# A decoder layer on eight cores: convolution chunks and the sample's pieces between attention steps, gate product first, squares on either engine

## The chip, the cores and the metric

The kernel runs as one program on the 8 cores of one Trainium2 chip. Each core takes one of the 8 prompts (2,048 tokens) and 16 of the 128 sample tokens, and holds its whole share of the work; the cores exchange nothing. The metric is the device time of the slowest core, in microseconds (us). Five engines of a core run side by side, each with an instruction list of its own: TensorE (PE: matmuls), ScalarE (ACT: functions such as Silu, Ln, Exp, Square, which need one of several function tables), VectorE (DVE), GpSimd (POOL: here it only issues the weights' DMAs) and SyncE (SP: issues the other DMAs). A semaphore orders one engine's work behind another's.

## What is computed

One layer, on the tokens of the prompt and on the sample's. `token_mixer` has a gated linear attention (GLA) with a 64x128 state per head, beside a short gated convolution:

```python
h = x + 0.5 * rms_norm(swiglu(rms_norm(x, ng[0]), f1_gate, f1_up, f1_down), ng[1])
mix, s_new, conv_new = token_mixer(rms_norm(h, ng[2]), s0, conv0, w_in, w_gate_up, b_gate,
                                   gla_norm_g, conv_w, w_out)
h = h + rms_norm(mix, ng[3])
h = h + 0.5 * rms_norm(swiglu(rms_norm(h, ng[4]), f2_gate, f2_up, f2_down), ng[5])
gate = jax.nn.sigmoid(rms_norm(h, ng[6]) @ w_ple_gate)
h = h + rms_norm((p @ w_ple_proj) * gate, ng[7])

# swiglu: (silu(x @ w_gate) * (x @ w_up)) @ w_down
# GLA per token: S_t = diag(a_t) S_{t-1} + k_t^T v_t, o_t = q_t S_t; the prompts start with S = 0
# conv group: cb * sum_j conv_w[j] * (cc * ch)[t - 2 + j]; out = concat(gla, conv) @ w_out
```

d_model is 1024, the swiglu's inner width 2816, 4 heads, all in float32. Outputs are h of prompt and sample and the new GLA and convolution states of both.

## The kernel before

**Tiles and streams.** Tokens lie along the free axis, channels along the 128 partitions. A core's 2,064 tokens are 6 tiles of 344, so a matmul of the big products is 128x128 by 344 columns. Two streams, A (tiles 0, 2, 4) and B (tiles 1, 3, 5), go through the stages at the same time, a pass being one tile of each; the names of their buffers end in A and B. The sample's 16 tokens are the last columns of tile 5, so stream B has them in the third pass.

**Stages of a tile.** ffn1 (`ffn`, f=0); the mixer (gates; convolution chunks `conv_chunk` 0 to 3; keys and queries; values; attention over three chunks of up to 128 tokens; output projection); ffn2 (`ffn`, f=1); the embedding stage (`ple`). Between stages stands `boundary` (L725): 8 norm-sum matmuls are closed, `rsq` makes 1/sqrt with an Ln and an Exp on ScalarE, `add_pair` adds the branch to h on VectorE (two operations on 688 columns), then for each pair of channel blocks a Square of h (688 columns) and two scalings with the norm's weights (344 columns each) run on ScalarE, and TensorE takes each pair as it comes (two sums with a matrix of ones `csr`, then its part of the next stage's first products, `feed`). `evac` (L768) empties a product's bank in the same way: Square, then Identity with a scale, both on ScalarE. In the embedding stage `xprep` prepares the next tile's x for its first norm (Square on ScalarE, scaling on VectorE) and TensorE sums its 8 squares with 8 matmuls.

**What sets the order.** The program is written by a planner that runs before the kernel is built. `P.op` puts work of ScalarE and VectorE on a list of pending operations; `pick` (L185) takes from it the one that its cost model would start first, with a surcharge (SWITCH) for a change of function table and the priority `P.prio` as tie break. The main loop (L1422) gives TensorE to the stream whose operands are planned to be there, with the streams' lead deciding ties. Where the planner sees TensorE idle for over 0.6 us it adds matmuls on constants, `warm` (L485), named `ps_bank<-sb_csr 128x344` and recorded at L496, 0.6 of the planned idle time at 0.157 us each. Their results are not used. Once written, each engine's order is fixed, and an instruction waits for its semaphores there.

**Weights.** Both streams use the same weights, which go through a ring in SBUF, `wring`: `pump` (L588) issues blocks from GpSimd in a fixed list (`ffn_w`, `mix_w`, `ple_w`) up to 20 ahead, and a block's place is free when the slower of the streams has released it. While the sample's GLA states lie in the ring (the list's last blocks of `mix_w`, `sg`), `S.pin` (L1095) keeps the ring from moving on.

**Start.** x of both tiles (`load_h`) and the constants (`ngl`, the norms' weights, among them) come over SP's queue; the third weight block waits for x (`gate0`). SP issues in the order in which the planner took them from the list.

**Attention and the sample.** For each chunk: `step_a` (scores: 4 matmuls, mask on VectorE, key transposes), `step_c` (outputs and the new state, which goes over ScalarE and VectorE into `Sr` and `Sst`), `step_d` (norm of the outputs). `gla_done` makes a stream's attention wait for the other's, as it takes over its state. One convolution chunk stands between steps of passes 1 and 2 and two after them. In the third pass all `2 * NS` pieces of `sample_gla` (L1181) come ahead of the first step: a piece is a group of small matmuls `sb_xnB,sb_sqB 128x256` (k times v of the sample) or `sb_WB,sb_wring 128x2` (q times the state), with VectorE's update of the state in the ring between them.

## Time and profile before

| | us |
|---|---|
| median of 3 runs | 1646.17 (1643.25 to 1696.57) |
| the profiled execution, device time | 1645.65 |
| its span, slowest core (core 1) | 1644.0 |
| spans of the 8 cores | 1631.0 to 1644.0 |

| engine | busy us | share | instructions |
|---|---|---|---|
| TensorE | 1537.0 | 93% | 9454 |
| ScalarE | 736.5 | 45% | 1437 |
| VectorE | 715.9 | 44% | 1421 |
| GpSimd | 268.5 | 16% | 512 |

How to read it: the span is the time from the first to the last instruction of the core with the trace shown, and the runs' times are those of the slowest core. The granted clock of TensorE is given as a share of full speed (2.4 GHz), averaged over a stretch; its two levels are 1.0 and half of that (1.2 GHz). A busy TensorE at half clock does half the work, so what a stretch loses is its idle time and, besides, its width times what the clock lacks of 1.

### The profile page before, as it was taken

Reading aid. Unit: us, or ns where it says so; the run is one execution under the profiler, and the core shown is the slowest. Engines: PE = TensorE matmul, PEld = TensorE weight load, DVE = VectorE, ACT = ScalarE, POOL = GpSimd, SP = SyncE. Lnnn points to the kernel's source line nnn. Section 1 sums busy time; section 2 is a strip of 40 time slices with the busy share of each in tenths; the row PEclk is TensorE's granted clock in tenths of the full one; section 3 lists DMA queues with packets and bytes.
Section 4 is the critical chain, followed back from the end, with each engine's and each line's share of the span. In section 5 each row is a group of like instructions: output and inputs, shape, how many; then the busy total and the mean of one; then the engine's idle time right before and its main releaser. Section 6 shows DMA issues by size and latency. Waiting matters only on the chain.

```text
span 1644.0 us, 27962 instructions; the slowest of 8 cores (1631.0 to 1644.0 us)
## 1 busy us (share of the span) xinstructions
PE 1537.0 (93%) x9454; PEld 1492.4 (91%) x9454; DVE 715.9 (44%) x1421; ACT 736.5 (45%) x1437; POOL 268.5 (16%) x512
## 2 busy tenths in 40 slices
PE   6999999899998999999989999799998998999996
PEld 5999889889997999989989999799998997889995
DVE  3331464543324643155554422573315754433136
ACT  3112665642147611275574124841138474511266
POOL 3211210112121221111112112022111110111110
PEclk9999999999998999998999999899999995999998
DMA  9865843468666796565446668399556443566661
GB/s 282 255 186 160 233 142 102 112 181 250 186 193 191 208 328 209 170 184 167 102 156 208 200 176 249 112 279 319 177 160 202 137 142 100 158 177 175 203 190 69
DMA packets 83452, 305.39 MB, mean 186 GB/s; under 512 B 9538, under 2 KB 12498, under 8 KB 82548
## 3 DMA queue, kind: packets, MB, share of 16 engines
q0 software_dynamic: 73040, 283.97, 58.4%
q1 hardware_dynamic: 10276, 19.65, 3.7%
q8 instruction: 80, 1.31, 0.3%
q14 instruction: 56, 0.46, 0.1%
HBM read 292.83 MB, written 10.75 MB: 185 GB/s over the span
## 4 chain that ended last, share of the span: by engine, by line
PE 79%; DMA 7%; ACT 6%; DVE 4%; issue 4%; DVEq 0%; SPq 0%; ACTq 0%; POOLq 0%; POOL 0%
PE ps_bank L472 78%; DMA sb_wring<-f2a 3%; DMA sb_wring<-f2b 2%; ACT L519 2%; DMA sb_wring<-f1b 1%; ACT sb_xnB L519 1%; DVE sb_hB L522 1%; DVE sb_xnB L522 1%; DMA sb_ngl<-ngl 1%; ACT sb_ta L519 1%; PE ps_bank L496 1%; ACT sb_WA L519 1%; PE ps_bank L504 0%; ACT sb_sqB L519 0%; DVE sb_WA L527 0%
## 5 line engine op out<-in xcount | busy, mean ns | idle before, releaser
L472 PE MATMUL ps_bank<-sb_xnA,sb_wring 128*128 128x344 f32 x2208 | 410.6, 332 | 19.0 <-DVE sb_WA L527 8.6
L472 PE MATMUL ps_bank<-sb_xnB,sb_wring 128*128 128x344 f32 x2208 | 396.6, 323 | 6.6 <-ACT sb_xnB L519 5.7
L472 PEld LDWEIGHTS ps_bank<-sb_xnA,sb_wring 128*128 128x128 f32 x2208 | 370.1, 197 | 27.2 <-issue 26.0
L472 PEld LDWEIGHTS ps_bank<-sb_xnB,sb_wring 128*128 128x128 f32 x2208 | 358.2, 190 | 13.5 <-issue 13.1
L472 PE MATMUL ps_bank<-sb_WA,sb_wring 128*128 128x344 f32 x1872 | 330.7, 323 | 11.4 <-DVE sb_WA L527 4.7
L472 PE MATMUL ps_bank<-sb_WB,sb_wring 128*128 128x344 f32 (+1 forms) x1904 | 333.7, 320 | 1.7 <-DVE sb_wring L522 1.0
L472 PEld LDWEIGHTS ps_bank<-sb_WA,sb_wring 128*128 128x128 f32 x1872 | 301.6, 189 | 17.8 <-issue 17.5
L472 PEld LDWEIGHTS ps_bank<-sb_WB,sb_wring 128*128 128x128 f32 x1904 | 309.1, 190 | 2.6 <-issue 2.4
L607 POOL DMA_DIRECT2D sb_wring<-f2a x132 | 69.7, 528 | 367.1 <-PE ps_bank L472 334.9
L519 ACT ACT_TABLE_LOAD x91 | 116.8, 1283 | 27.4 <-DMA sb_ngl<-ngl 14.4
L607 POOL DMA_DIRECT2D sb_wring<-f1a x132 | 69.7, 535 | 290.7 <-PE ps_bank L472 280.7
L519 ACT ACTIVATE sb_tg0A<-sb_tg0A 128x344 f32<-128x344 f32 x78 | 38.2, 490 | 158.5 <-DVE sb_tg0A L522 158.1
L519 ACT ACTIVATE sb_tg1A<-sb_tg1A 128x344 f32<-128x344 f32 x78 | 38.2, 490 | 155.9 <-DVE sb_tg1A L522 155.7
L522 DVE TENSOR_TENSOR sb_tg1A<-ps_bank,sb_rsA 128x344 f32<-128x344 f32 x84 | 43.3, 516 | 120.0 <-PE ps_bank L472 109.0
L522 DVE TENSOR_TENSOR sb_tg0A<-ps_bank,sb_rsA 128x344 f32<-128x344 f32 x84 | 43.3, 515 | 110.7 <-PE ps_bank L472 110.6
L519 ACT ACTIVATE sb_sqA<-ps_bank 128x344 fp32r<-128x344 f32 x72 | 32.9, 457 | 119.0 <-PE ps_bank L472 118.7
L519 ACT ACTIVATE sb_tg0B<-sb_tg0B 128x344 f32<-128x344 f32 x78 | 38.2, 490 | 97.6 <-DVE sb_tg0B L522 97.6
L519 ACT ACTIVATE sb_sqB<-ps_bank 128x344 fp32r<-128x344 f32 x72 | 32.7, 455 | 99.1 <-PE ps_bank L472 93.5
L522 DVE TENSOR_TENSOR sb_sqA<-sb_sqA 128x344 fp32r<-128x344 f32 x36 | 18.6, 518 | 126.6 <-ACT sb_sqA L519 125.1
L472 PE MATMUL ps_bank<-sb_sqB,sb_csr 128*128 128x344 f32 (+2 forms) x155 | 47.7, 353 | 26.4 <-ACT sb_sqB L519 12.3
L519 ACT ACTIVATE sb_tg1B<-sb_tg1B 128x344 f32<-128x344 f32 x78 | 38.3, 491 | 69.9 <-DVE sb_tg1B L522 69.8
L522 DVE TENSOR_TENSOR sb_sqB<-sb_sqB 128x344 fp32r<-128x344 f32 x36 | 18.6, 517 | 107.6 <-ACT sb_sqB L519 106.6
(198 smaller groups left out, 1647.6 us busy)
## 6 DMA issues: line engine op xcount, KB each, us to landing
sb_wring<-f1a POOLq DMA_DIRECT2D x132, 512.0 KB, 10.0
sb_wring<-f2a POOLq DMA_DIRECT2D x132, 512.0 KB, 5.5
sb_wring<-f1b POOLq DMA_DIRECT2D x48, 704.0 KB, 5.5
sb_wring<-f2b POOLq DMA_DIRECT2D x48, 704.0 KB, 5.3
sb_wring<-wca POOLq DMA_DIRECT2D x24, 512.0 KB, 6.8
sb_wring<-wo POOLq DMA_DIRECT2D x24, 512.0 KB, 5.6
sb_wring<-wpg POOLq DMA_DIRECT2D x24, 512.0 KB, 7.3
sb_wring<-wg POOLq DMA_DIRECT2D x12, 512.0 KB, 6.7
```

Source lines behind the costliest of these rows:

```text
L472: ins = e.matmul(out.ap, a.ap, b.ap, start=(first and i == 0), stop=(last and i == n_ - 1))
L496: ins = e.matmul(out.ap, a.ap, b.ap, start=True, stop=True)
L519: P.op("act", lambda e: e.activation(out=out.ap, in_=in_.ap, func=func, **kw), reads=rd, writes=[out], table=table)
L522: P.op(eng, lambda e: e.tensor_tensor(out=out.ap, in0=in0.ap, in1=in1.ap, op=op), reads=[in0, in1], writes=[out])
L607: P.op("pool", (lambda o, s: lambda e: e.dma_start(out=o.ap, in_=s))(dst, src), reads=gate0 if i == 2 else (), writes=[dst], dma=f"ws{i % ...
```

## The change

**Who does a square or a scaling.** An operation on the pending list may have two ways, on ScalarE or VectorE (`sqr`, `scl`). The planner takes the way that starts first by its model, with a term `late` for the later one. `boundary`, `evac`, the first norm, the convolution's first tap and `xprep` use them. Exp with scale -0.5, the second half of each 1/sqrt, gets 20 more priority (`PAIR`), so that it follows its Ln more closely.

**Order of products.** In `ffn` the gate's product is first and the up product second, and the gate's own operations are pending before the up product is issued. In the mixer the values come ahead of keys and queries (the `vrow` block is moved up as it is); `mix_w` has the blocks in the new order; one buffer (`Einv`) and the softplus values (`sps`) move to other places.

**Between attention steps.** Convolution chunk 1 leaves its place ahead of the keys, so that three chunks (1 to 3) stand between the attention steps or right behind; in the third pass all three stand ahead of the attention. Of the sample's pieces one (`FIRST`) is done before the wait for `gla_done` and up to 6 (`EACH`) in each of the attention's steps. What `sample_gla` keeps moves from `sq` to a free part of `xn`.

**Sums of x.** `xprep` adds its squares in pairs on VectorE, and TensorE sums 2 vectors per tile and not 8. **Start.** What is pending is written out before the constants are asked for, and the planner's model has a transfer time for SP's large loads.

```diff
+FIRST = 1
+EACH = 6
+PAIR = 20.0
...
+                o.due = [self.ready(w[0], o.reads, o.writes) for w in o.ways]
+            for way, (eng, fn, kw) in enumerate(o.ways):
+                due, free = o.due[way], self.free[eng]
+                t = max(due, free)
+                tab = kw.get("table")
+                turn = SWITCH if tab is not None and tab != self.table else 0.0
+                late = max(0.0, t - min(max(d, self.free[w[0]]) for d, w in zip(o.due, o.ways)))
+                key = (t + turn if due > free + 0.15 else free, due - o.prio + turn + late)
+                if best is None or key < best[0]:
+                    best = (key, t, o, way)
...
+            elif writes and ndma == 1 and width > 400:
+                self.link = max(self.link, start + 2.0) + 0.0018 * width
+                self.done[tok] = self.link + 0.5
...
+            if func == AF.Exp and scale == -0.5:
+                P.prio += PAIR
...
+        def sqr(out, in_):
+            P.op("act", lambda e: e.activation(out=out.ap, in_=in_.ap, func=AF.Square), reads=[in_], writes=[out],
+                 other=("dve", lambda e: e.tensor_tensor(out=out.ap, in0=in_.ap, in1=in_.ap, op=ALU.mult), {}))
+
+        def scl(out, in_, g):
+            P.op("act", lambda e: e.activation(out=out.ap, in_=in_.ap, func=AF.Identity, scale=g.ap), reads=[in_, g], writes=[out],
+                 other=("dve", lambda e: e.tensor_scalar(out=out.ap, in0=in_.ap, scalar1=g.ap, scalar2=None, op0=ALU.mult), {"dur": 0.4}))
...
         def mix_w(smp):
             o = halves(wg_d, 0) + halves(wg_d, 1)
-            for c in range(2):
-                o += halves(wca_d, c) + [(wcb_d, c, 0, 1024)]
+            o += halves(wca_d, 0) + [(wcb_d, 0, 0, 1024)]
+            o += [(wv_d, 0, 0, 2048), (wv_d, 1, 0, 2048)]
             o += halves(wkq_d, 0) + halves(wkq_d, 1)
-            o += [(wv_d, 0, 0, 2048), (wv_d, 1, 0, 2048)]
-            for c in range(2, 4):
+            for c in range(1, 4):
...
-                act(q, hp, AF.Square)
+                sqr(q, hp)
                 for k in range(2):
-                    act(xv(S, c + k, n), hv(S, c + k, n), AF.Identity, scale=gvec(gpre, c + k))
+                    scl(xv(S, c + k, n), hv(S, c + k, n), gvec(gpre, c + k))
...
-            act(raw(S, m, n), bank.v(0, n), AF.Identity, scale=gvec(g, m, half))
+            scl(raw(S, m, n), bank.v(0, n), gvec(g, m, half))
...
-                bu_ = yield from prod(S, n, fA_d[f], j, 1024)
                 bg_ = yield from prod(S, n, fA_d[f], j, 0)
...
+                later(gate)
+                bu_ = yield from prod(S, n, fA_d[f], j, 1024)
+
...
-            yield from conv_chunk(S, T, 1)
...
             if last_pass:
-                for c in range(2, 4):
+                for c in range(1, 4):
                     yield from conv_chunk(S, T, c)
...
-            done_c = 4 if last_pass else 2
+            done_c = 4 if last_pass else 1
...
             if ns:
-                go = True
-                for _ in range(2 * NS):
-                    if go:
-                        go = yield from piece()
-            prev = None
+                for _ in range(FIRST):
+                    go = yield from piece()
+            while T.idx > 0 and not gla_done[T.idx - 1]:
+                yield None
             for s in range(nch):
-                lo, hi = T.chunks[s]
-                yield pe([wv_(S, T, "kt", 0, 2 * n), wv_(S, T, "qtz", 0, 4 * n)])
-                am = step_a(s)
+                yield from prep(s)
                 if prev is not None:
                     step_d(*prev)
                 if done_c < 4:
                     yield from conv_chunk(S, T, done_c)
                     done_c += 1
-                yield pe([am.v(0, 512), W.v(o["kz"], o["kz"] + 512), Sr[gk["k"] % 2].v(0, 256)])
-                bo, oq = step_c(s, am)
+                for _ in range(EACH):
+                    if go:
+                        go = yield from piece()
+                kb, k0 = kz_at(s)
+                yield pe([ams[s], kb.v(k0, k0 + 512), Sr[gk["k"] % 2].v(0, 256)])
+                bo, oq = step_c(s, ams[s])
                 prev = (s, bo, oq)
+            while go:
+                go = yield from piece()
             for c in range(done_c, 4):
...
-            kept = S.sq.v(0, 512, 0, NS, r=True)
+            kept = S.xn.v(2048, 2560, 0, NS, r=True)
...
-                q = S.W.v((18 + c % 4) * n, (19 + c % 4) * n, r=True)
-                act(q, xr, AF.Square)
-                ts(S.W.v((10 + c) * n, (11 + c) * n, r=True), xr, gvec(0, c), None, ALU.mult, None)
-                xq.append(q)
+                k = 18 + c if c < 2 else 20 + c % 2
+                sqr(S.W.v(k * n, (k + 1) * n, r=True), xr)
+                scl(S.W.v((10 + c) * n, (11 + c) * n, r=True), xr, gvec(0, c))
+                if c % 2 and c > 1:
+                    acc = S.W.v(18 * n, 20 * n)
+                    tt(S.W.v(18 * n, 20 * n, r=True), acc, S.W.v(20 * n, 22 * n), ALU.add)
 
...
+            xq = [S.W.v((18 + k) * n, (19 + k) * n, r=True) for k in range(2)]
+            bx = yield from hold()
             yield pe(xq, [bx.v(0, n)], True)
-            xsum(0)
+            mm(bx.v(0, n), [(csr.v(C_OD, C_OD + 128, r=True), q) for q in xq])
...
             load_h(streams[0], tiles[0], c)
+        P.settle(list(P.pending))
```

SyncE's list at its beginning (`hA`, `hB` are x of the two streams' first tiles, four loads each of two channel blocks). Before:

```order
L462 DMA sb_hB<-x 128x688 x4
L462 DMA sb_ngl<-ngl 128x64
L462 DMA sb_hA<-x 128x688 x4
L462 DMA sb_cst<-cst 128x392
L462 DMA sb_sm<-sm 128x16
```

Of the change:

```order
L475 DMA sb_ngl<-ngl 128x64
L475 DMA sb_hA<-x 128x688 x4
L475 DMA sb_hB<-x 128x688 x4
L475 DMA sb_cst<-cst 128x392
L475 DMA sb_sm<-sm 128x16
```

The norm's weights `ngl` are now first and stream A's x is ahead of stream B's; what follows is unmoved.

TensorE's list in the third pass, at the end of the sample's pieces and the beginning of an attention step of stream B (`WB` holds its keys and queries, `Sr` the state, `sqB` the masked scores or the sample's keys). Before:

```order
L472 MATMUL ps_bank<-sb_WB,sb_wring 128x2 x4
L472 MATMUL ps_bank<-sb_xnB,sb_sqB 128x256 x4
L496 MATMUL ps_bank<-sb_csr 128x344 x2
L472 MATMUL ps_bank<-sb_WB,sb_wring 128x2 x4
L472 MATMUL ps_bank<-sb_xnB,sb_csr 128x64
L472 MATMUL ps_bank<-sb_WB 128x128 x4
L504 MATMUL ps_bank<-sb_cst,sb_WB 128x128 x2
L472 MATMUL ps_bank<-sb_WB,sb_Sr 128x128
L472 MATMUL ps_bank<-sb_sqB,sb_WB 128x128
```

Of the change, around a piece in the middle of the attention:

```order
L485 MATMUL ps_bank<-sb_WA,sb_wring 128x344 x8
L485 MATMUL ps_bank<-sb_sqA,sb_csr 128x344
L485 MATMUL ps_bank<-sb_WA,sb_wring 128x344 x8
L485 MATMUL ps_bank<-sb_WB,sb_wring 128x2 x4
L485 MATMUL ps_bank<-sb_xnB 128x256 x4
L485 MATMUL ps_bank<-sb_sqA,sb_csr 128x344 x2
L509 MATMUL ps_bank<-sb_csr 128x344 x4
L485 MATMUL ps_bank<-sb_WB,sb_wring 128x2 x4
L485 MATMUL ps_bank<-sb_WB,sb_Sr 128x128
L485 MATMUL ps_bank<-sb_sqB,sb_WB 128x128
```

Before, the pieces stand one behind the other, with fillers (`sb_csr`) between, and then the attention steps. Now stream A's full products (`sb_WA,sb_wring 128x344`) stand between the pieces and the steps.

TensorE's list where stream B goes from ffn2 to the embedding stage for the first time, while stream A is in that stage (`xnB` is the scaled h). Before:

```order
L472 MATMUL ps_bank<-sb_xnA,sb_wring 128x344 x8
L496 MATMUL ps_bank<-sb_csr 128x344 x2
L472 MATMUL ps_bank<-sb_sqA,sb_csr 128x344
L472 MATMUL ps_bank<-sb_WA,sb_csr 128x344
L472 MATMUL ps_bank<-sb_WA,sb_wring 128x344 x2
L472 MATMUL ps_bank<-sb_xnA,sb_wring 128x344 x8
L472 MATMUL ps_bank<-sb_sqA,sb_csr 128x344
L472 MATMUL ps_bank<-sb_WA,sb_csr 128x344
L472 MATMUL ps_bank<-sb_sqB,sb_csr 128x344 x2
L472 MATMUL ps_bank<-sb_xnB,sb_wring 128x344 x2
```

Of the change:

```order
L485 MATMUL ps_bank<-sb_xnA,sb_wring 128x344 x8
L485 MATMUL ps_bank<-sb_sqA,sb_csr 128x344
L509 MATMUL ps_bank<-sb_csr 128x344 x15
L485 MATMUL ps_bank<-sb_sqB,sb_csr 128x344 x2
L485 MATMUL ps_bank<-sb_xnB,sb_wring 128x344 x4
L509 MATMUL ps_bank<-sb_csr 128x344 x6
L485 MATMUL ps_bank<-sb_sqB,sb_csr 128x344 x2
L485 MATMUL ps_bank<-sb_xnB,sb_wring 128x344 x4
L509 MATMUL ps_bank<-sb_csr 128x344 x3
```

Before, four of A's product groups stand in B's passage and two fillers; now fillers do (15, 6 and 3), A's groups follow, and one of A's norm matmuls (`sb_WA,sb_csr`) of each pair is gone with the sums of x.

## Rows read from the trace of the kernel before

**Rows 1.** The page's part 1: busy us, share of the span, instructions.

```profile
PE 1537.0 (93%) x9454; PEld 1492.4 (91%) x9454; DVE 715.9 (44%) x1421; ACT 736.5 (45%) x1437; POOL 268.5 (16%) x512
```

**Rows 2.** Core 1, TensorE by windows: us, busy (instructions), clock, DMA, GB/s.

```profile
0.00:20.00 20.00, 3.88 (x11) 1.00 0.87 242
200.00:260.00 60.00, 54.28 (x334) 0.94 0.45 131
280.00:360.00 80.00, 71.27 (x418) 0.94 0.48 143
500.00:560.00 60.00, 51.31 (x275) 0.89 0.52 164
720.00:760.00 40.00, 34.41 (x185) 0.87 0.40 126
780.00:860.00 80.00, 73.38 (x494) 1.00 0.43 121
1020.00:1060.00 40.00, 30.53 (x158) 0.87 0.51 166
1240.00:1280.00 40.00, 35.17 (x198) 0.91 0.49 155
1340.00:1400.00 60.00, 53.57 (x248) 0.66 0.33 100
1420.00:1560.00 140.00, 132.45 (x817) 1.00 0.62 177
```

**Rows 3.** Timeline, start: start us, us, what [idle before <-releaser].

```profile
2.90 0.85 SPq L462 DMA_DIRECT2D sb_ngl<-ngl  x1
...
12.84 6.87 POOL L607 DMA_DIRECT2D sb_wring<-f1a  x13 [9.57 <-DMA sb_hB<-x]
...
14.40 1.28 ACT L519 ACT_TABLE_LOAD   x1 [14.40 <-DMA sb_ngl<-ngl]
...
16.37 0.63 PE L472 MATMUL ps_bank<-sb_sqA,sb_csr 128*128 128x344 f32 x1 [7.97 <-DVE sb_sqA L522]
```

**Rows 4.** Groups by line, ScalarE and VectorE: busy us, mean ns | idle before.

```profile
L519 ACT ACT_TABLE_LOAD x91 | 116.8, 1283 | 27.4 <-DMA sb_ngl<-ngl 14.4 <-PE ps_bank L472 3.6 <-DVE sb_tg1B L522 3.3
...
L519 ACT ACTIVATE sb_xnB<-sb_hB,sb_ngl 128x344 fp32r<-128x344 f32 x80 | 42.0, 568 | 0.0
...
L519 ACT ACTIVATE sb_sqB<-sb_hB 128x688 fp32r<-128x688 f32 x36 | 27.7, 769 | 3.3 <-DVE sb_hB L522 3.2
...
L522 DVE TENSOR_TENSOR sb_hB<-sb_hB,sb_xnB 128x688 f32<-128x688 f32 x28 | 24.1, 871 | 0.7
...
L534 DVE TENSOR_SCALAR sb_WB<-sb_WB,sb_ngl 128x344 fp32r<-128x344 f32 x16 | 6.3, 395 | 2.8 <-ACT sb_WB L519 2.7
```

**Rows 5.** Timeline, TensorE, first passage from ffn2 to the embedding stage.

```profile
506.65 0.83 PE L472 MATMUL ps_bank<-sb_WA,sb_wring 128*128 128x344 f32 x2 [2.34 <-DVE sb_WA L527]
...
513.84 0.55 PE L472 MATMUL ps_bank<-sb_sqB,sb_csr 128*128 128x344 f32 x2 [1.31 <-ACT sb_sqB L519]
...
527.97 2.63 PE L472 MATMUL ps_bank<-sb_xnA,sb_wring 128*128 128x344 f32 x8 [3.14 <-DVE sb_WA L527]
```

**Rows 6.** Timeline, ScalarE, a table load there and the next activation.

```profile
504.03 1.28 ACT L519 ACT_TABLE_LOAD   x1
...
505.33 0.49 ACT L519 ACTIVATE sb_tg1A<-sb_tg1A 128x344 f32<-128x344 f32 x1
```

**Rows 7.** Timeline, TensorE, the attention step behind the sample's pieces.

```profile
1384.71 0.45 PE L472 MATMUL ps_bank<-sb_WB,sb_Sr 128*128 128x128 f32 x1 [2.07 <-ACT sb_Sr L519]
...
1386.44 1.49 PE L472 MATMUL ps_bank<-sb_WB 128*128 128x128 f32 x8
```

**Rows 8.** Timeline, TensorE, the same kind of step in the first pass.

```profile
289.50 0.22 PE L472 MATMUL ps_bank<-sb_WB,sb_Sr 128*128 128x128 f32 x1
...
290.34 0.61 PE L472 MATMUL ps_bank<-sb_WB 128*128 128x128 f32 x4
```

**Rows 9.** The page's part 5: issues of one kind of weight block, GpSimd.

```profile
L607 POOL DMA_DIRECT2D sb_wring<-f2a x132 | 69.7, 528 | 367.1 <-PE ps_bank L472 334.9
```

126 lines of the change are left out of this document (63 added, 63 removed).

## The prediction

> **What bounds the kernel now.** I read the page's table of engines first. TensorE is busy 1537.0 us in a span of 1644.0, ScalarE and VectorE under half of it [rows 1]. So the kernel is bound by TensorE's work, and what an edit can win is what TensorE loses: its idle time, and what its clock lacks. Full-speed work is already dense: in the long ffn stretch of the last pass 817 matmuls take 132.45 us, 0.162 us each, at clock 1.00 [rows 2].
>
> Then I went through the span in windows and took for each (width - busy) + (1 - clock) x width. The losses lie at few places [rows 2]:
>
> - start, 0 to 20: 20 - 3.88 = 16.1.
> - ffn1 to mixer, three passes (200:260, 720:760, 1240:1280): 5.7 + 3.6, 5.6 + 5.2, 4.8 + 3.6 = 28.5.
> - mixer to ffn2, two passes (280:360, 780:860): 8.7 + 4.8, and 6.6 = 20.1.
> - ffn2 to embedding, two passes (500:560, 1020:1060): 8.7 + 6.6, 9.5 + 5.2 = 30.0.
> - the sample, 1340:1400: 6.4 idle + 0.34 x 60 = 20.4 of clock = 26.8.
> - 1420:1560: 7.5, idle alone, at full clock.
>
> Together 129 us. The timeline of TensorE then tells what ends its waits. In the passage to the embedding stage it waits 2.34, 1.31 and 3.14 us for products and squares on VectorE and ScalarE [rows 5]: a serial chain through both engines, during which ScalarE also changes its function table. At the start the first product waits for x: GpSimd's issues go on at 12.84, behind `hB`; the norm weights `ngl`, issued at 2.90 behind `hB`, let ScalarE begin at 14.40; TensorE starts at 16.37 [rows 3].
>
> **The change, part by part.** Durations come from the profiled execution, so the sum is made against its 1645.65 us (span 1644.0 and 1.65 around it), 0.5 under the median shown, 1646.17.
>
> *Two ways for squares and scalings.* From the two programs' lists: ScalarE's activations fall from 1348 to 1112, VectorE's operations rise from 1423 to 1671. In the lists the function table changes 69 times where it did 91, as Exp now follows its Ln. That is 22 x 1.283 = 28 us less of loads on ScalarE [rows 4]. In a passage (four Squares of 688 columns and eight scalings) ScalarE now needs 4 x 0.77 + 8 x 0.57 = 7.6 us. A pair on VectorE costs 0.87 for the square (two operands, as the 688-column add) and 0.40 per scaling, against 0.77 and 0.57 [rows 4]. Shared between both, a passage's preparation could end 2 to 3 us earlier. But VectorE also has `add_pair` there, 2 x 0.87 x 4 = 7 us, which stands ahead of the squares in the same passage. So I take a good third of the loss at each place: 8.5 of 28.5 at ffn1 to mixer (2.8 a passage), 5 of 20.1 at mixer to ffn2. Bounds: 0 (VectorE's adds set the pace anyway) and 24 (half of both).
>
> *The passage to the embedding stage.* The lists show opposite things. A's norm sums of x shrink: 32 matmuls become 8 over four tiles, 24 x 0.16 = 3.8 us of certain work. But A's groups no longer stand in B's passage; 24 fillers do, which are 24 x 0.162 = 3.9 us of matmuls that compute nothing, written for a planned gap of 24 x 0.157 / 0.6 = 6.3 us. Before, the waits of 2.34, 1.31, 3.14 and shorter ones made 8.7 [rows 2, 5]. So the idle time hardly shrinks, while the fillers hold the clock, of which 6.6 and 5.2 us are lost today [rows 2]. I take 2 us a passage, 4, beside the 3.8. Bounds: 0 and 12.
>
> A rule of the Trainium skill speaks for more. "ScalarE: Activation LUTs", section "What ACT_TABLE_LOAD costs", puts a switch at some 1283 ns for the load plus some 1380 ns of drain. By it 22 fewer switches would be 58 us of ScalarE and not 28. The trace agrees with the first figure and shows no drain of this size: a load begins at 504.03, lasts 1.28, and the next activation starts at 505.33 [rows 6]. By the page's figure the gain at the passages would lie nearer its bound of 24, by the row it stays at 13.5.
>
> *The sample.* Before, all pieces stand in a row, with small matmuls and fillers, and TensorE's clock is at 0.66 over 60 us; the attention's step behind them waits 2.07 us for the state and runs its 8 small matmuls in 1386.44 - 1384.71 = 1.73 us, at half clock, where the same step in pass 1 takes 290.34 - 289.50 = 0.84 [rows 2, 7, 8]. Now A's full products stand between pieces and steps. The waits (2.07 here and a few of 0.5 to 1.3) should mostly go: 4 of the 6.4 idle. Of the clock's 20.4 I take a third, 7: the pieces are still many small matmuls. Sum 11. Bounds: 4, and 20. Three convolution chunks between the attention's steps in passes 1 and 2 fill waits of the same kind; they are in the 5 above.
>
> *The start.* `ngl` first and `hA` ahead of `hB` lets A's norm begin some us sooner. But weight blocks 1 and 2 and the x of both tiles share the same link (DMA share 0.87 over 0:20 [rows 2]), and GpSimd's third block waits for `hB`, which lands later now, so what is won on A is partly lost on the weights. I take 5. Bounds: 0 and 8 (16.37 minus the about 8 us that ngl and A's x need at 242 GB/s: 1.4 MB, 5.8 us, behind an issue at 1 us).
>
> *Gate ahead of up, values ahead of keys.* The same matmuls in another order. Silu gets one product's time (8 x 0.16 = 1.3 us) more; in the dense stretches nothing waits for it, so 0. If that cover is gone (a tight ring of buffers), each costs at most its 0.5 us of Silu. The values need only `xn`, and their evacuation stands in the time in which keys and queries wait for the gates: in the 5 above.
>
> *Fillers.* Their count rises from 121 to 157: 36 x 0.162 = 5.8 us of TensorE. A filler in a true gap is free; where the operands come earlier than planned it delays. I charge half: +3. Bounds 0 and 5.8.
>
> Sum: -5 - 8.5 - 5 - 4 - 3.8 - 11 + 3 = -34.3; 1645.65 - 34.3 = 1611.4, rounded to 1612.
>
> **The rivals.**
>
> 1. *Relief that is off the path.* ScalarE and VectorE are under half busy [rows 1], so less of ScalarE's time need not shorten a chain that goes through both: VectorE's `add_pair` of 7 us sets the pace of a passage, and the stalls move to it. Then of the two-ways edit a quarter is left (3.4 of 13.5), the passage to the embedding stage keeps only its 3.8 less 3 of fillers, the sample gives its waits and little of the clock (6), the start 3: 1645.65 - 3.4 - 0.8 - 6 - 3 = 1632.5. For it speaks that the planner itself still plans 24 fillers into one passage. Against it: TensorE's waits name ScalarE's squares and scalings too [rows 5]. 0.32.
>
> 2. *The clock stays up.* In all windows above the clock's lack is 3.6 + 5.2 + 3.6 + 4.8 + 6.6 + 5.2 + 20.4 = 49.4 us. If fewer and filled gaps keep TensorE at its upper level nearly everywhere, half of this comes back and not the 13 or so that my sum has in it: 12 more and all table relief converts, 10 more: 1590. 0.12.
>
> 3. *VectorE becomes the bound of the passages (slower).* The two ways move onto VectorE some 29 squares of 688 columns and 56 scalings of h: 29 x 0.87 + 56 x 0.40 = 47.6 us, over 18 passages 2.6 each. The planner chooses by its own model of both engines; if the moved work stands ahead of `add_pair` of the other stream or of the gates' products, all of it is on the path: 1645.65 + 47.6 less 13 (start 5, and 8 of the sample) = 1680. It decides when over 46 of the 47.6 us are on the path, so 0.04.
>
> 4. *Weights come late.* The mechanism would be that a scaling on VectorE holds GpSimd's next issue back. Scalings of this kind, SBUF to SBUF, rise from 33 to 87 by the lists; if each held back an issue by its 0.40 us [rows 4], that is 54 x 0.40 = 21.6 us at most, and 1612 + 10 = 1622 if half of them met an issue that TensorE waits for. In the trace the issues take 528 ns on average, and GpSimd's idle time before them is 367 us, 335 of it waiting for TensorE to free the ring [rows 9]: slack. So 0.05. A rule of the Trainium skill stands behind this rival and speaks against the change: "SBUF — State Buffer", section "Who interferes with whom", says that a VectorE tensor_scalar in its two-port mode takes the port pair that it shares with GpSimd, and GpSimd is locked out for the whole instruction. No row of before shows such a lock.
>
> **How the numbers follow.** Main case 0.47 (its own range 1598 to 1625), rival 1 0.32 (1624 to 1642), rival 2 0.12 (1585 to 1598), rival 4 0.05, rival 3 0.04. The predicted time is 1612. The range of 1592 to 1638 leaves out rival 3, the lower half of rival 2 and the top quarter of rival 1, under 0.2. 2% is about what a measurement of this kernel can tell from no change; it lies at 0.98 x 1646.17 = 1613.2. The main case is a little over half below it (0.27), rival 2 all (0.12), rival 4 hardly (0.01): faster 0.40. Only rival 3 reaches 1679, mostly: slower 0.03. Same 0.57.
>
> **What would show it.** In the new profile: TensorE's first product at 11 to 12 us (start). Table loads 69, 89 us in all. The windows at the three kinds of passage with 2 to 3 us less idle time and VectorE busy in them; if the waits there are now for VectorE's `hB` and `xnB`, rival 1 holds. In the sample's part no wait of 2 us for `Sr`, and a clock over 0.75; if it is 0.66 still, 7 us of the sum are missing. Passages to the embedding stage with clock 1.00 and about 8 us of idle and fillers. Waits for `wring` longer than before would show rival 4. The forecast is wrong if the busy time of TensorE doesn't fall, though its waits do: then the clock gave nothing back.

## The result, and the profile after

The changed kernel is slower: 1657.03 us (median of 6 runs) where the kernel before has 1647.38 beside it, ratio 1.0061 with a 95% interval of 1.0039 to 1.0082. That is 10 us more where the prediction had 34 less. The interval is clear of 1, so this is a small loss and not a tie, though one of less than 2%. Its profiled execution has a span of 1651.3 us (core 7). All ratios are taken over the runs in which neither half of the chip ran at a lower clock than the other; e16 and e17 below have no such runs, and for them I give the ratio of cores 0 to 3 alone.

The page's line of engines, of the changed kernel:

```profile
PE 1540.8 (93%) x9466; PEld 1494.7 (91%) x9466; DVE 850.3 (51%) x1669; ACT 603.7 (37%) x1179; POOL 268.9 (16%) x512
```

Beside [rows 1], ScalarE has 133 us less and VectorE 134 us more: the work moved as the lists said. TensorE's busy time (1537.0 before, 1540.8 now) and share did not fall, and nor did all its waits together (88.1 us before, 92.1 now, median of the cores).

TensorE in the windows of [rows 2], of the changed kernel (us, busy, instructions, clock, DMA share, GB/s):

```profile
0.00:20.00 20.00, 7.13 (x23) 1.00 0.80 219
200.00:260.00 60.00, 55.05 (x358) 0.91 0.44 128
280.00:360.00 80.00, 71.63 (x425) 0.94 0.51 150
500.00:560.00 60.00, 54.88 (x327) 0.97 0.70 198
720.00:760.00 40.00, 33.25 (x170) 0.74 0.43 128
780.00:860.00 80.00, 72.72 (x447) 0.94 0.41 109
1020.00:1060.00 40.00, 33.64 (x194) 1.00 0.71 212
1240.00:1280.00 40.00, 32.53 (x163) 0.78 0.46 146
1340.00:1400.00 60.00, 53.53 (x297) 0.86 0.32 93
```

The same account as in the prediction, idle time and clock together, before against after: passages to the embedding stage (500:560, 1020:1060) 30.0 against 5.1 + 1.8 + 6.4 = 13.3. Passages from ffn1 to the mixer (200:260, 720:760, 1240:1280) 28.5 against 10.4 + 17.2 + 16.3 = 43.9. Mixer to ffn2 (280:360, 780:860) 20.1 against 13.2 + 12.1 = 25.3. The sample's window 26.8 against 14.9. By these windows the passages to the embedding stage gained 16.7 us, about twice the 7.8 of the forecast, and the passages around the mixer lost where a gain was forecast.

Fixed windows are blind to work that moves over their edge. So I also took, on all 8 cores, the times at which TensorE issues its n-th 344-column matmul of a weight block (8160 in either kernel), at places where both kernels have done the same work, and the median over the cores of the width of each part:

| from, to (n-th) | what | before | changed | e1: passages on ScalarE |
|---|---|---|---|---|
| 0, 80 | start | 34.4 | 33.3 | 34.5 |
| 960, 1760 | mixer, pass 1 | 190.9 | 194.9 | 191.0 |
| 2560, 2880 | to embedding, pass 1 | 72.9 | 68.8 | 65.9 |
| 3760, 4400 | mixer, pass 2 | 159.7 | 170.9 | 159.8 |
| 5200, 5520 | to embedding, pass 2 | 76.8 | 72.1 | 67.4 |
| 6400, 7120 | mixer and sample, pass 3 | 208.7 | 209.1 | 205.6 |
| 7920, 8159 | end | 51.2 | 54.9 | 50.5 |

The parts left out differ by 1.1 us at most. The loss is in the mixers' passages of passes 1 and 2 (+4.0, +11.2) and at the end (+3.7). The passages to the embedding stage gained 4.1 and 4.7, which is 8.8 and not the 16.7 of the windows. The sample's pass is as long as before: what its window shows as a gain was given back beside it.

What TensorE waits for, in all, of the changed kernel (engine, line waited for: us in total, times, longest):

```profile
PE ps_bank L485 <- DVE sb_sqB L557: 14.7, 8, 3.2
PE ps_bank L485 <- ACT sb_sqB L556: 9.9, 8, 2.0
PE ps_bank L485 <- DVE sb_WA L544: 9.7, 6, 2.7
PE ps_bank L485 <- DVE sb_WB L539: 9.0, 5, 2.1
```

L557 is the VectorE way of `sqr`. Before, the passages had no such wait, and now it is the largest. VectorE's timeline in the second pass's passage from ffn1 to the mixer shows how it comes (changed kernel, core 7):

```profile
719.86 0.87 DVE L539 TENSOR_TENSOR sb_WB<-sb_WB,sb_rqB 128x688 fp32r<-128x688 f32 x1
721.21 0.88 DVE L539 TENSOR_TENSOR sb_hB<-sb_hB,sb_WB 128x688 f32<-128x688 f32 x1 [0.47 <-DVE sb_WB L539]
722.26 0.88 DVE L557 TENSOR_TENSOR sb_sqB<-sb_hB 128x688 fp32r<-128x688 f32 x1 [0.17 <-DVE sb_hB L539]
723.05 0.39 DVE L561 TENSOR_SCALAR sb_xnB<-sb_hB,sb_ngl 128x344 fp32r<-128x344 f32 x1
723.36 2.44 DVE L539 TENSOR_TENSOR sb_WB<-sb_WB,sb_rqB 128x688 fp32r<-128x688 f32 x3
725.72 0.87 DVE L539 TENSOR_TENSOR sb_hB<-sb_hB,sb_WB 128x688 f32<-128x688 f32 x1
726.69 0.88 DVE L557 TENSOR_TENSOR sb_sqB<-sb_hB 128x688 fp32r<-128x688 f32 x1
...
727.91 1.64 DVE L539 TENSOR_TENSOR sb_hB<-sb_hB,sb_WB 128x688 f32<-128x688 f32 x2
```

A square, a scaling and three multiplies stand between the first and the second add to h (the second add needs one of these multiplies), another square between the second and the third. From the first multiply to the last add it takes 729.55 - 719.86 = 9.7 us. The same passage of the kernel before (core 1), first and last row:

```profile
728.90 0.88 DVE L522 TENSOR_TENSOR sb_WB<-sb_WB,sb_rqB 128x688 fp32r<-128x688 f32 x1 [0.69 <-ACT sb_rqB L519]
...
735.69 0.86 DVE L522 TENSOR_TENSOR sb_hB<-sb_hB,sb_WB 128x688 f32<-128x688 f32 x1
```

There it is 736.55 - 728.90 = 7.65 us, with two multiplies and nothing else between the first and the second add. Over all 18 passages of a core, the mean time from the first add to the end of the last is 6.4 us before and 8.3 in the change (median of the cores). What the new order does to the other two engines, changed kernel, ScalarE and then TensorE:

```profile
726.68 1.05 ACT L560 ACTIVATE sb_xnB<-sb_hB,sb_ngl 128x344 fp32r<-128x344 f32 x2 [3.92 <-DVE sb_hB L539]
...
728.91 0.78 ACT L556 ACTIVATE sb_sqB<-sb_hB 128x688 fp32r<-128x688 f32 x1 [1.18 <-DVE sb_hB L539]
```

```profile
723.28 0.91 PE L485 MATMUL ps_bank<-sb_sqB,sb_csr 128*128 128x344 f32 x2 [2.15 <-DVE sb_sqB L557]
...
727.71 0.91 PE L485 MATMUL ps_bank<-sb_sqB,sb_csr 128*128 128x344 f32 x2 [2.37 <-DVE sb_sqB L557]
```

ScalarE, which could have done the square, is idle for 3.92 us because the next h isn't there, and TensorE waits twice, 4.5 us together. Its clock falls with the first of these gaps to the lower level, stays there through the second, and falls once more ten us later (window, busy, instructions, clock, DMA share, GB/s):

```profile
720.00:723.00 3.00, 1.14 (x8) 1.00 1.07 294
723.00:737.00 14.00, 11.32 (x37) 0.51 0.23 78
737.00:747.00 10.00, 8.22 (x54) 1.00 0.43 134
747.00:754.00 7.00, 6.58 (x25) 0.52 0.32 101
```

The mean over 720:760 is 0.74, where it was 0.87.

### The profile page after: what moved, and what is told of

Its sections match the earlier page's. It is cut to its first block, busy times and chain, and to the rows that moved or that the text cites. A ratio compares the mean times of both kernels' runs of the same rounds, so it can differ in the third digit from the quotient of the medians.

```text
span 1651.3 us, 28350 instructions; the slowest of 8 cores (1637.0 to 1651.3 us)
## 1 busy us (share of the span) xinstructions
PE 1540.8 (93%) x9466; PEld 1494.7 (91%) x9466; DVE 850.3 (51%) x1669; ACT 603.7 (37%) x1179; POOL 268.9 (16%) x512
## 4 chain that ended last, share of the span: by engine, by line
PE 79%; DVE 9%; issue 4%; DMA 4%; ACT 3%; DVEq 0%; POOL 0%; ACTq 0%; POOLq 0%
PE ps_bank L485 78%; DVE sb_hB L539 1%; DMA sb_wring<-f2a 1%; DMA sb_wring<-f1b 1%; PE ps_bank L509 1%; DVE sb_xnB L539 1%; DMA sb_wring<-f1a 1%; DVE sb_hA L539 1%; DMA sb_wring<-f2b 1%; DVE sb_tb L544 1%; ACT L535 1%; DVE sb_sqB L557 1%; DVE sb_WB L539 1%; DVE sb_xnB L561 0%; DMA sb_wring<-wpg 0%
## 5 line engine op out<-in xcount | busy, mean ns | idle before, releaser
L485 PE MATMUL ps_bank<-sb_xnA,sb_wring 128*128 128x344 f32 x2208 | 402.7, 327 | 26.4 <-DVE sb_WA L544 8.2
L485 PE MATMUL ps_bank<-sb_xnB,sb_wring 128*128 128x344 f32 x2208 | 406.0, 328 | 4.9 <-DVE sb_WB L544 2.3
L485 PEld LDWEIGHTS ps_bank<-sb_xnA,sb_wring 128*128 128x128 f32 x2208 | 364.2, 193 | 35.5 <-issue 35.0
L485 PEld LDWEIGHTS ps_bank<-sb_xnB,sb_wring 128*128 128x128 f32 x2208 | 367.5, 194 | 9.9 <-issue 9.6
L535 ACT ACT_TABLE_LOAD x68 | 87.2, 1283 | 9.2 <-PE ps_bank L485 4.5
L485 PE MATMUL ps_bank<-sb_sqB,sb_csr 128*128 128x344 f32 (+2 forms) x155 | 51.7, 382 | 33.3 <-DVE sb_sqB L557 14.7
L539 DVE TENSOR_TENSOR sb_tg1B<-ps_bank,sb_rsB 128x344 f32<-128x344 f32 x84 | 43.2, 515 | 60.7 <-PE ps_bank L485 51.0
L539 DVE TENSOR_TENSOR sb_tg0B<-ps_bank,sb_rsB 128x344 f32<-128x344 f32 x84 | 43.2, 514 | 56.3 <-PE ps_bank L485 52.6
L485 PEld LDWEIGHTS ps_bank<-sb_sqB,sb_csr 128*128 128x128 f32 x155 | 29.7, 210 | 44.8 <-issue 44.4
```

The costliest lines, as they stand in the source:

```text
L485: ins = e.matmul(out.ap, a.ap, b.ap, start=(first and i == 0), stop=(last and i == n_ - 1))
L535: P.op("act", lambda e: e.activation(out=out.ap, in_=in_.ap, func=func, **kw), reads=rd, writes=[out], table=table)
L539: P.op(eng, lambda e: e.tensor_tensor(out=out.ap, in0=in0.ap, in1=in1.ap, op=op), reads=[in0, in1], writes=[out])
```

## The experiments

All ratios are to the kernel before, run beside each on the same chip. A hundredth is 16.5 us, and the intervals are about 0.002 (3 us) either way. First, what the loss is.

**e1, passages on ScalarE alone.**

```diff
-                sqr(q, hp)
+                act(q, hp, AF.Square)
...
-                    scl(xv(S, c + k, n), hv(S, c + k, n), gvec(gpre, c + k))
+                    act(xv(S, c + k, n), hv(S, c + k, n), AF.Identity, scale=gvec(gpre, c + k))
```

> The changed kernel with one part undone: in the passages between stages (boundary) squares and scalings are on ScalarE alone, as before; the two ways stay everywhere else. Theory 1 (VectorE's squares and scalings stand between its own adds to h, so the next pair comes later and TensorE waits 2 to 3 us for sqB on VectorE, then runs at half clock): the 14.7 us of waits for VectorE's sqB go, and about 15 us of the changed kernel's 1657, so 1636 to 1645, ratio to before 0.993 to 0.999. Theory 2 (the new order of the mixer costs the time, whoever squares): no more than 3 us better, 1654 to 1657. Theory 3 (the relief of ScalarE was worth something in the passages and is now missing): slower than the change, 1660 to 1665.

Measured: 1624.55 us, ratio 0.9854 (0.9834 to 0.9874). These calls in `boundary` make 34 us (0.0207 of ratio), more than twice the 14.7 us of waits for VectorE's `sqB`. Other waits come on top (all of TensorE's waits are 92.1 us in the change and 75.1 in e1, median of the cores), and the clock behind the gaps. The rest of the change is worth 24 us of gain. The third column of the table has where: 11 us in pass 2's mixer, 3 to 5 in each of pass 1's and pass 3's and in either passage to the embedding stage, 4 at the end.

**e2, no operation with two ways at all.** `sqr` and `scl` call ScalarE; the first norm's squares and the scaling of the next x are on VectorE, as before.

> The changed kernel without any operation of two ways: every square and scaling goes to the engine that had it before (ScalarE in passages, evacuations and convolution; VectorE for the first norm's squares and the scaling of the next x). All else as in the change. Theory 1: the gain comes from the passages alone, so this is within 4 us of the kernel with the passages alone undone: 1636 to 1648. Theory 2: 1654 to 1657. If the two ways are worth something outside the passages (evacuations, x), this one is slower than the passages alone undone, by up to 8 us.

Measured: 1622.84, ratio 0.9872 (0.9832 to 0.9913). The two ways are worth nothing that can be told in the evacuations and the rest either, and no harm of theirs shows outside the passages.

**e5, the two ways of the passages alone, put into the kernel before.**

> The kernel before with one part of the change alone: squares and scalings of the passages between stages have two ways. Theory 1 (the two ways in the passages are the loss, in whatever kernel they stand; taking them out of the changed kernel gave 32 us): 15 to 32 us slower than before, 1662 to 1679, ratio 1.009 to 1.02. Theory 1b (the loss needs the change's other parts, for instance gates that come onto VectorE earlier): within 5 us of before, 1643 to 1653.

Measured: 1652.42, ratio 1.0029 (1.0013 to 1.0045). A loss, but 5 us and not 34: theory 1b. In this kernel's list 25 of the squares and 33 of the scalings stand between the first and the last add of their passage, as many as in the changed kernel (19 and 40). The adds take as long as there, too: the mean from the first add to the end of the last is 8.4 us, against 6.4 in the kernel before. So neither the count of these operations nor the longer row of adds fixes the price.

**e6, squares with two ways, scalings on ScalarE.**

> The changed kernel with the passages' scalings on ScalarE alone; their squares keep two ways. Theory 1a (the square on VectorE, 0.87 us of the engine that also adds to h, is what delays the next pair): most of the loss stays, 1645 to 1657. Theory 1c (the scalings, eight of 0.40 us a passage, fill VectorE): most of it goes, 1625 to 1635.

Measured: 1647.71, ratio 0.9994 (0.9978 to 1.001). Between both: of the 34 us, the squares alone keep 23, and 11 need the scalings.

**e7, the adds to h first.** Everything keeps two ways, and only the priority of the adds changes:

```diff
-                P.prio = URGE + 8 - c
+                P.prio = URGE + 28 - c
                 add_pair(c)
```

> The changed kernel with both ways kept everywhere, and 20 more priority for the adds to h in a passage (add_pair), so that no square or scaling stands on VectorE ahead of an add that could run. Theory 1 in its strict form (the squares are harmful because of their place ahead of the adds, not because they are on VectorE): 1620 to 1632, as the kernel with the ways undone. If the occupancy of VectorE does it, in whatever order: 1640 to 1657.

Measured: 1629.43, ratio 0.9888 (0.9861 to 0.9915), 28 us better than the change. The passage of above, VectorE (core 0):

```profile
717.76 0.88 DVE L539 TENSOR_TENSOR sb_WB<-sb_WB,sb_rqB 128x688 fp32r<-128x688 f32 x1
718.75 0.88 DVE L539 TENSOR_TENSOR sb_hB<-sb_hB,sb_WB 128x688 f32<-128x688 f32 x1
719.54 1.65 DVE L539 TENSOR_TENSOR sb_WB<-sb_WB,sb_rqB 128x688 fp32r<-128x688 f32 x2
721.11 0.87 DVE L539 TENSOR_TENSOR sb_hB<-sb_hB,sb_WB 128x688 f32<-128x688 f32 x1
721.89 0.87 DVE L539 TENSOR_TENSOR sb_WB<-sb_WB,sb_rqB 128x688 fp32r<-128x688 f32 x1
722.68 1.66 DVE L539 TENSOR_TENSOR sb_hB<-sb_hB,sb_WB 128x688 f32<-128x688 f32 x2
```

No square stands between the adds, and the chain takes 724.34 - 717.76 = 6.6 us and not 9.7. But the run does not part the place from the number. With the adds first the planner also gave work back to ScalarE: 9 of the passages' squares are on VectorE where the change has 29, and 40 scalings where it has 56, and VectorE is 829.2 us busy and not 850.3. That the place makes most of the harm is likely, since e5 has 36 squares and 50 scalings on VectorE and loses 5 us, but it is not shown: e5 has as many of them between the adds as well.

**e13, the same priority in the kernel before.** It asks whether e7's gain is that of the priority in itself.

> The kernel before with 20 more priority for the adds to h in the passages, nothing else; its squares and scalings are on ScalarE. If the 27 us of the same edit in the changed kernel came from adds that no longer stand behind squares and scalings on VectorE: little is to be had here, 1641 to 1648. If the priority in itself is worth it (adds behind the other stream's work): 1620 to 1630.

Measured: 1639.97, ratio 0.995 (0.9929 to 0.997). So 8 us of such a gain have nothing to do with squares on VectorE: before, adds also stood behind the other stream's work. If the parts add up, some 20 of e7's 28 us belong to the squares and scalings. Beside the change's other parts the priority by itself brings nothing certain (e15 below beside e8), and then their share is larger.

Second, where the 24 us of gain of the rest come from. These start at e1's kernel (0.9854) and undo one part more, or add one part to the kernel before.

**e9, the old sums of the next x** (8 matmuls per tile, their bank of PSUM held from the stage's beginning, the squares on ScalarE and the scalings on VectorE again).

> The changed kernel with the passages on ScalarE alone, and besides with the old sums of the next x: Square on ScalarE, scaling on VectorE, 8 matmuls with the ones matrix per tile instead of 2. The kernel beside it has 1624.5; between it and the kernel before, 16 of 24 us lie in the two passages from ffn2 to the embedding stage, where this work stands. If the smaller sums and the shared squares bring those 16: 1640. If they are worth their 24 matmuls alone, 3.8 us: 1628. If nothing: 1624.

Measured: 1634.22, ratio 0.9917 (0.9902 to 0.9933): 10 us. In the two passages to the embedding stage the widths go from 65.9 to 72.7 and from 67.4 to 74.3.

**e14, the new sums alone in the kernel before.**

```diff
-                while len(xq) > keep:
-                    mm(bx.v(0, n), [(csr.v(C_OD, C_OD + 128, r=True), xq.pop(0))], xseen[0] == 0, xseen[0] == 7)
...
+                if c % 2 and c > 1:
+                    acc = S.W.v(18 * n, 20 * n)
+                    tt(S.W.v(18 * n, 20 * n, r=True), acc, S.W.v(20 * n, 22 * n), ALU.add)
```

> The kernel before with the new sums of the next x alone (added in pairs on VectorE, 2 matmuls per tile and the bank held only at the end), each operation on its old engine. In the mended kernel going back to the old sums cost 10 us, 13.7 of it in the two passages from ffn2 to the embedding stage. If the sums are the gain by themselves: 1633 to 1640, ratio 0.991 to 0.995. If they need the other parts: 1645 to 1649.

Measured: 1631.29, ratio 0.9871 (0.9848 to 0.9894): 21 us by themselves, nearly as much as the 24 of all the rest. But it is not the same gain. In e14 the passages to the embedding stage are 3.4 and 5.8 us shorter than before (69.5 and 71.0), and pass 2's mixer is 7.6 shorter (152.1). In e1 the passages are 7.0 and 9.4 shorter, and pass 2's mixer is as long as before (159.8); in e9, with the old sums, it takes 154.6. So the sums are worth 10 us by e9 and 21 by e14.

**e18, the same, but the bank held from the stage's beginning.**

```diff
+            if N is not None:
+                bx = yield from hold()
...
-            bx = yield from hold()
```

> The kernel before with the new sums of x alone, but with their bank of PSUM held from the beginning of the embedding stage, as before. The same kernel that takes the bank at the end has 1631.3, the kernel before 1650, ratio 0.987. If the bank makes the gain: 1643 to 1650, ratio 0.996 to 1. If the 24 matmuls and the fewer waits for squares make it: 1630 to 1635, ratio 0.987 to 0.99.

Measured: 1641.01, ratio 0.9962 (0.9941 to 0.9983). e16 is the same kernel and has 0.996 on cores 0 to 3. So 15 of the 21 us are there only if the bank is taken late, and 6 come from the matmuls and the rest. What the bank does is less clear than that. Of the 15 us, 9.2 lie in pass 2's mixer (161.3 in e18, 152.1 in e14), where no stream holds `bx`, and only 1.6 and 0.7 in the two passages. In that mixer the planner wrote another order for e14, with 8 fillers where e18 and the kernel before have 25 and the same order as each other. So part of the price is the plan that follows from the edit, and not the wait for a bank. What TensorE waits for in 490:560, of the kernel before, of e14 and of e18:

```profile
PE ps_bank L472 <- DVE sb_WA L527: 5.5, 2, 3.1
```

```profile
PE ps_bank L472 <- ACT sb_sqB L519: 7.3, 1, 7.3
PE ps_bank L472 <- DVE sb_WB L527: 0.9, 1, 0.9
```

```profile
PE ps_bank L472 <- DVE sb_WA L527: 5.7, 3, 2.6
```

The wait for `sb_WA L527` is there when the bank is held and gone when it isn't; in e14 one wait of 7.3 us for a square stands in its place, and all waits of the window together are no fewer. Of the two groups of matmuls that wait in [rows 5], one (`sb_xnA,sb_wring`) doesn't read `WA`, and the other reads only the part of it that a DMA fills (`p`). L527 is the operation of `ple` that reads a product's bank last; it gives the bank free. Over the whole run this kind of wait (medians of the 8 cores) is 14.1 us before, 9.0 in e18, 6.0 in e14; 6.6 in e1, 13.1 in e9. And it is 12.6 in the changed kernel, which has the free bank; that VectorE, busy with squares, comes late to empty the banks there is my reading and was not tested. All waits of TensorE together are 88.1 us before, 82.1 in e18 and 82.2 in e14.

**e3 and e8, the mixer's old order**, in the changed kernel and in e1's.

> The changed kernel with the mixer's old order: values behind keys and queries, convolution chunk 1 ahead of them, two chunks between the attention's steps, weights in that order; the sample's pieces stay spread, the two ways stay. Theory 2 (the new mixer order costs the time): 10 us or more better than the change, 1640 to 1647. Theory 1: the passages' waits stay, within 4 us of the change, 1653 to 1661.

> The changed kernel with the passages on ScalarE alone, and besides with the mixer's old order (values behind keys and queries, chunk 1 ahead of them, two chunks between attention steps). The kernel it stands beside, with the passages alone undone, has 1624.5. If the mixer's order is worth what it was beside the two ways (1663.5 against 1657.0), this is 6 us slower: 1631, ratio 0.990. If it is worth the 5 us that the prediction had, 1629. If it is worth nothing once the passages are mended: 1624.

Measured: 1663.49, ratio 1.008 (1.0061 to 1.01), beside 1.0061 of the change; and 1622.52, ratio 0.9848 (0.9821 to 0.9875), beside 0.9854. Values first and three chunks between the attention's steps move nothing that can be told.

**e4 and e12, all pieces of the sample first**, in the same two.

```diff
-FIRST = 1
-EACH = 6
+FIRST = 32
+EACH = 0
```

> The changed kernel with all the sample's pieces ahead of the first attention step, as before (32 pieces first, none between). The prediction had 11 us of gain for spreading them; the trace of the changed kernel shows the third pass's mixer no shorter (209.1 us against 208.7), with 7 us less lost to the clock and 5 more idle. If spreading is worth what the clock gave (7 us): 1664, ratio 1.010. If spreading is worth nothing: 1657, ratio 1.006. If it costs: 1652.

> The changed kernel with the passages on ScalarE alone, and besides all the sample's pieces ahead of the attention, as before. Beside the two ways the old place cost 3 us (1660.0 against 1657.0), where the prediction had 11 of gain for the new one. If it is 3 again: 1627.5. If the gain of 11 had been hidden behind the waits for VectorE: 1635.

Measured: 1660.02, ratio 1.0068 (1.0047 to 1.0089), and 1622.69, ratio 0.9865 (0.9843 to 0.9887): within 2 us of their neighbours, with intervals of 3 us. The widths of pass 3's mixer are 209.1 with the pieces spread and 215.0 with them first in the change, but 205.6 and 207.7 in e1's kernel. The clock's loss there is 14.6 us spread and 17.2 with the pieces first in the change, 16.4 and 14.5 in e1's kernel (medians of the cores): that spread pieces keep the clock up can't be told from this.

**e10 and e11, no priority for the Exp; the up product first.**

> The changed kernel with the passages on ScalarE alone, and besides PAIR at 0, so that an Exp has no priority behind its Ln. If the fewer table loads (each 1.283 us of ScalarE) bring the gain of the passages from ffn2 to the embedding stage: 1632 to 1640. If ScalarE's time is off the path: within 3 us of 1624.5.

> The changed kernel with the passages on ScalarE alone, and besides with the up product ahead of the gate's in both ffn, as before. The prediction had 0 for this part: 1624.5 within 3 us. If the gate ahead gives Silu the time it needs at the passages (the first products behind a passage wait for it): 1628 to 1636.

Measured: 1624.9, ratio 0.9869 (0.9851 to 0.9888): the priority brings nothing that can be told. The run says nothing of the table loads, since it has as many as e1. First e1, then e10:

```profile
L535 ACT ACT_TABLE_LOAD x76 | 97.5, 1283 | 11.2 <-PE ps_bank L485 6.6 <-DVE sb_tg1A L539 1.8 <-DVE sb_tg1B L539 1.5
```

```profile
L535 ACT ACT_TABLE_LOAD x76 | 97.5, 1283 | 14.0 <-PE ps_bank L485 6.4 <-DVE sb_tg1A L539 4.0 <-DVE sb_tg1B L539 2.3
```

For e11, the up product first, 1627.43, ratio 0.9884 (0.9868 to 0.9899): the gate ahead brings some 5 us beside e1's 0.9854, at the edge of what the intervals allow.

**e15, ScalarE in the passages, the mixer's old order and the adds first.**

> The changed kernel with the passages on ScalarE alone, the mixer's old order, and the adds first. If the adds' priority only undoes what squares on VectorE did, it adds nothing to the 1622.5 of the same kernel without it: 1620 to 1625. If it is worth something in itself: 1612 to 1619.

Measured: 1621.83, ratio 0.9833 (0.9814 to 0.9853). The fastest kernel of the study, 28 us ahead of the kernel before and 37 ahead of the change; beside e8 (0.9848) the adds' priority adds nothing certain.

## Why the prediction was wrong, step by step

**The two ways in the passages: the step that failed, and it failed in sign.** I had 13.5 us of gain, since ScalarE's share of a passage (7.6 us) would be split. I had written beside it that VectorE has `add_pair` there, 7 us, "which stands ahead of the squares in the same passage", and took that as a reason to count only a third of the gain. The adds do not all stand ahead. The planner puts the square of the first pair on VectorE as soon as its h is there, and the second pair's add behind it, so that the next h, both engines' work on it and TensorE's sums come later, and TensorE waits for `sqB` (14.7 us, 8 times) where no such wait was. The order of VectorE's list showed that (19 squares and 40 scalings between first and last add) and I read only the counts of operations from it. The measured price is 34 us (e1). Rival 3 came nearest, with VectorE as the pace and 47.6 us of moved work, though it had that work ahead of the other stream's adds and the timeline shows it ahead of the stream's own. I gave it 0.04 because I asked for nearly all of that work on the path.

**The likeliest case came true by luck.** I gave 0.57 to a time within 2% of the kernel before, and that is where it lies. But the forecast had no loss in it that a gain would nearly cancel: the rest, taken for 34.3 - 13.5 = 20.8 us of gain, gave 24, its single parts being off by more than that, and the part taken for 13.5 cost 34.

**What stays open there.** The same edit costs 34 us in the changed kernel and 5 in the kernel before, with as many squares between adds. The trace has a candidate: VectorE, when late, also frees the banks late (12.6 us of such waits in the change, 6.6 in e1), and in the kernel before those waits are there anyway (14.1). This is argued from the waits and was not tested apart. Two other differences are as open: e5 has 79 table loads where the kernel before has 91, and every edit lets the planner write another order far from the place of the edit, as e14 and e18 show.

**The passage to the embedding stage: right place, mis-sized.** I had 3.8 for the matmuls and 4 for the passage. The two passages gained 8.8 in the change and 16.4 in e1, and the sums of x alone measured 10 (e9) to 21 (e14). I took the waits of 2.34 and 3.14 for `WA` as a chain through squares and products. By the code they are waits for a bank: `bx` was held through the whole stage, by each stream, out of six that both share. That `bx` is now taken at the end is in the diff, and my sum had no term for it; by e18 it is the larger part of the 21, though most of it shows in pass 2's mixer.

**Table loads.** The count was right, 68 and 1 loads in the changed kernel:

```profile
L535 ACT ACT_TABLE_LOAD x68 | 87.2, 1283 | 9.2 <-PE ps_bank L485 4.5 <-DVE sb_tg1B L539 2.3 <-DVE sb_tg1A L539 1.3
```

What 28 us less of ScalarE are worth was not measured apart: no run changes the number of loads alone. They are not what makes the gain, since e1 has 77 loads and is 34 us faster than the change with its 69. That fits rival 1, relief off the path. The Trainium skill ("ScalarE: Activation LUTs", "What ACT_TABLE_LOAD costs") gives some 2.66 us for a switch, with some 1380 ns of drain beside the load. The trace agrees with the load's 1283 ns and shows no such drain, here as before:

```profile
719.78 1.28 ACT L535 ACT_TABLE_LOAD   x1
721.07 0.49 ACT L535 ACTIVATE sb_WA<-sb_tg1A 128x344 fp32r<-128x344 f32 x1
```

**The sample: failed.** 11 us forecast, 0 to 2 measured (e4, e12). The wait of 2.07 for `Sr` is gone, as said, and the clock in its window is 0.86 and not 0.66. But the third pass's mixer takes 209.1 us where it took 208.7. Over the whole of it the clock's loss fell from 21.9 to 14.6 us, much as the 7 in my sum, and the idle time, of which I had taken 4 off, rose from 14.1 to 19.2 (medians of the cores): other waits came. So the term for the waits failed. And the gain of clock is not clearly the spreading's, as e4 and e12 show. A window around the old place sees the gain and not what was pushed out of it.

**The mixer to ffn2, values first, three chunks: failed by its 5 us,** which are among the 13.5 above. The new order of the mixer brings nothing that can be told by e3 and e8.

**The start.** 5 us forecast, 1.1 seen up to the 80th matmul (table above). Changed kernel, core 7:

```profile
6.11 0.63 PE L485 MATMUL ps_bank<-sb_sqA,sb_csr 128*128 128x344 f32 x1 [6.11 <-DVE sb_sqA L557]
10.05 0.63 PE L485 MATMUL ps_bank<-sb_xnA,sb_wring 128*128 128x344 f32 x1 [3.31 <-DMA sb_wring<-f1a]
14.13 0.62 PE L485 MATMUL ps_bank<-sb_xnA,sb_wring 128*128 128x344 f32 x1 [3.45 <-DMA sb_wring<-f1a]
19.38 6.87 POOL L631 DMA_DIRECT2D sb_wring<-f1a  x13 [16.09 <-DMA sb_hB<-x]
```

Stream A's first sum stands at 6.11 and not at 16.37 [rows 3]. Then TensorE waits 3.31 and 3.45 us for the first two weight blocks, which GpSimd issued at 2.22, nearly as before; that they share the link with x I had named. The loss that I had named is there, since the third block waits for `hB` and goes out at 19.38 and not at 12.84, but TensorE does not wait for that block. Up to 19.4 the pairs of wide matmuls take 0.78 us and from 19.96 on 0.48, so this work runs at the lower level of the clock, whatever the 1.00 of the row 0:20 says. e17 takes e1's kernel and undoes the new order of the loads: 0.9895 on cores 0 to 3, where e1 has 0.9855 on the same cores, some 7 us slower. So beside the other parts the new order is worth about what I forecast, and against the kernel before nearly nothing of it is left; why was not found out.

**Gate first.** 0 forecast, some 5 measured (e11).

**Weights late, rival 4: no price seen.** Of the changed kernel:

```profile
L631 POOL DMA_DIRECT2D sb_wring<-f2a x132 | 69.7, 528 | 351.9 <-PE ps_bank L485 333.7
```

The issues take 528 ns as in [rows 9], with 56 scalings of h more on VectorE. TensorE's wait for `f2a` fell from 6.2 to 4.3 us (medians of the cores). The Trainium skill ("SBUF — State Buffer", "Who interferes with whom") speaks of a lock between a VectorE tensor_scalar in its two-port mode and GpSimd. The mean shows none. On the 8 cores together, the 74 issues of `f1a` and `f2a` that overlap a scaling from SBUF take 582 ns on average, up to 680, and the others 533; in the kernel before it is 533 and 532. So if there is a lock, it costs GpSimd under 1 us a core here.

**Fillers.** +3 forecast. The 15 in the passage to the embedding stage run for 3.86 us. The planner put them in a gap that it had planned; what they cost was not measured apart:

```profile
508.46 3.86 PE L509 MATMUL ps_bank<-sb_csr 128*128 128x344 f32 x15
```

So it was a change of two large parts: +34 us for the two ways in the passages, and -24 for all the rest, of which the sums of x are -10 to -21. I had the first as -13.5 and the sums with their passage as -7.8.

## What to carry to other kernels

Before you give an operation two engines, look in the new order for what stands between the links of the serial chain on the engine that receives the work, and give those links priority first: here two engines brought nothing anywhere, and cost 34 us where the moved work stood between the links. A wait that names an operation whose result the waiting matmul does not read can be a wait for the buffer that this operation frees; find who holds the other buffers. Price every change of a `hold`, not only of instructions, and judge a local edit at points where both programs have done the same work, since a window at the old place sees only what left it. And where a planner writes the order, look at the places far from the edit too before you give the edit the credit.

## What the runs showed of the hardware

A gap in TensorE's work can cost more than itself: with the two waits of 2.15 and 2.37 us the clock fell, and the matmuls of 723:737 ran at 1.2 GHz, some 7 us lost. With a second stretch at that level (747:754) the window 720:760 loses 6.8 us of idle time and 10.4 of clock. Not every gap does so: the window 500:560 has a wait of 2.69 us and loses 1.8 us of clock. In the sample the clock did not clearly follow how the small matmuls are spread: 16.4 us of loss in pass 3's mixer spread and 14.5 in a row (e1, e12), but 14.6 and 17.2 in the change and e4. Scaling a bank of PSUM costs VectorE 576 ns for 344 columns (x32, changed kernel), against 395 from SBUF [rows 4].
